# The context tile taken out of the nine-tile gather loop and run first: a hybrid mixer and expert-retrieval step on one Trainium2 core

## The reference, cut to what matters

```
m = silu(cond) @ w_mod + b_mod           # six vectors sh1, sc1, g1, sh2, sc2, g2; cond is c_ctx or c
h = rmsnorm(x, norm1) * (1 + sc1) + sh1
mix:  z = h @ w_in                       # q, f_fw, f_bw, v, g, xr, xg (512 each), ga, gb (1024 each)
      A: 4 heads, chunks of 32 tokens, forward and backward: S_t = diag(f_t) S_{t-1} + k_t v_t^T, o_t = S_t^T q_t
      B: short convolution and gated linear recurrence, forward and backward
      merged = sigmoid(ga) * (A @ w_branch_a) + sigmoid(gb) * (B @ w_branch_b);  mix = merged @ w_out
x1 = x + g1 * mix
h2 = rmsnorm(x1, norm2) * (1 + sc2) + sh2
peer: queries h2 @ w_q for 8 heads x 2 halves; scores against 128 keys each; top 16 of each half,
      top 16 of the 256 sums -> 16 experts a head, 128 rows a token, of 16384;  gate = softmax of the best sums
      act = gelu(h2 . u[e]);  out = sum_e gate_e * act_e * v[e]
y = rmsnorm(x1 + g2 * out, norm_f)
```

## Time and profile before

| | us |
|---|---|
| median of 3 runs | 4078.19 (4070.95 to 4082.48) |
| the profiled execution, its own time | 4086.17 |
| its span, first to last instruction | 4084.3 |
| end of the norm chain, start of the heads' loop on TensorE | 54.5 |
| end of the fourth head's scan, start of the merge | 735.5 |
| first gather of expert rows | 958.7 |
| last gather issued | 4057.7 |

### The profile page before, as it was taken

One profiled execution on the slowest core, in us unless ns is written; L12 is line 12 of the kernel. 1 busy time (PEld: TensorE's weight loads), 2 busy tenths in 40 slices (PEclk: granted clock), 3 DMA queues, 4 the chain that ended last, 5 costly groups with the idle time before them and its releaser, 6 DMA issues.

```text
span 4084.3 us, 44739 instructions
## 1 busy us (share of the span) xinstructions
PE 3031.6 (74%) x15406; PEld 1311.9 (32%) x15406; DVE 2613.3 (64%) x6282; ACT 1069.5 (26%) x2720; POOL 1343.0 (33%) x1174
## 2 busy tenths in 40 slices
PE   8999999798689999785666656665665665665555
PEld 3767767444344444221121111111111111111111
DVE  4545455666467667564787766776776776676555
ACT  2534435002123333111232222222222222221111
POOL 0000000002233444342444444444444444444443
PEclk9999999898899999897888877878878878787777
DMA  4010000557899999999999999999999999999998
GB/s 178 22 31 18 28 16 1 219 177 285 340 387 385 405 416 402 419 407 421 417 404 417 419 407 418 416 418 412 419 414 410 418 416 401 420 417 399 420 420 346
DMA packets 214316, 1346.40 MB, mean 330 GB/s; under 512 B 24738, under 2 KB 45730, under 8 KB 63170
## 3 DMA queue, kind: packets, MB, share of 16 engines
q0 software_dynamic: 165888, 1208.03, 71.9%
q1 hardware_dynamic: 48196, 135.41, 8.8%
HBM read 1329.69 MB, written 13.67 MB: 329 GB/s over the span
## 4 chain that ended last, share of the span: by engine, by line
PE 39%; DMA 38%; DVE 13%; issue 5%; ACT 3%; POOL 2%; POOLq 0%; SPq 0%; DVEq 0%; ACTq 0%
DMA arena<-in_uv,mask_b 13%; PE ps L760 13%; DMA arena<-in_uv,mask_f 10%; DMA arena<-in_uv,ones 10%; PE ps L1420 9%; DVE arena L1275 6%; PE ps L738 4%; PE ps L621 3%; DMA arena<-in_w_q 2%; POOL arena L599 2%; ACT arena L957 2%; PE ps L1464 2%; PE ps L1414 2%; PE ps L1481 1%; PE ps L680 1%
## 5 line engine op out<-in xcount | busy, mean ns | idle before, releaser
L760 PE MATMUL ps<-arena 64*64 64x512 f32 x9216 | 1451.7, 757 | 936.2 <-ACT arena L957 888.2
L1275 DVE CUSTOM_DVE_ANT_0 arena<-arena 128x1024 f32<-128x1024 f32 x1152 | 1412.6, 1226 | 954.5 <-DMA arena<-in_uv,mask_b 363.0
L760 PEld LDWEIGHTS ps<-arena 64*64 64x64 f32 x9216 | 350.7, 158 | 1906.2 <-ACT arena L957 1362.3
L957 ACT ACTIVATE arena<-arena 128x64 f32<-128x64 f32 x1152 | 338.2, 341 | 1411.5 <-DVE arena L1154 1411.5
L599 POOL DMA_INDIRECT arena<-in_uv,ones x384 | 449.3, 1170 | 659.7 <-PE ps L760 491.8
L599 POOL DMA_INDIRECT arena<-in_uv,mask_f x384 | 445.2, 1159 | 581.2 <-PE ps L760 493.6
L599 POOL DMA_INDIRECT arena<-in_uv,mask_b x384 | 442.3, 1152 | 584.9 <-PE ps L760 491.8
L1420 PE MATMUL ps<-arena 128*128 128x384 f32 x1152 | 387.9, 493 | 15.4 <-issue 13.5
L953 ACT ACTIVATE arena<-arena 128x2 f32<-128x2 f32 x576 | 117.5, 204 | 859.1 <-DVE arena L1275 858.4
L583 POOL IOTA arena<- 128x16 f32 x1 | 0.1, 145 | 889.5 <-PE ps L630 889.5
L738 PE MATMUL ps<-arena 128*128 128x384 f32 x768 | 270.3, 499 | 0.0
(11 more groups left out here) (205 smaller groups left out, 2836.1 us busy)
## 6 DMA issues: line engine op xcount, KB each, us to landing
arena<-in_w_mod SPq DMA_DIRECT2D x12, 2048.0 KB, 23.3
arena<-in_w_mg SPq DMA_DIRECT2D x16, 1536.0 KB, 21.8
arena<-in_w_in SPq DMA_DIRECT2D x28, 512.0 KB, 3.4
arena<-in_w_out SPq DMA_DIRECT2D x2, 4096.0 KB, 18.1
arena<-in_w_q SPq DMA_DIRECT2D x8, 1024.0 KB, 20.8
arena<-in_w_q SPq DMA_DIRECT2D x4, 2048.0 KB, 33.6
arena<-x_scratch SPq DMA_DIRECT2D x15, 512.0 KB, 11.3
arena<-in_uv,ones POOLq DMA_INDIRECT x384, 10.5
```

Source lines behind the costliest of these rows:

```text
L760: mm = nc.tensor.matmul(PS[c * HALF:(c + 1) * HALF, 2 * r + n, :], DG[rows, s, :], RG[s][rows, D + n * 512:D + (n + 1) * 512], start=(g == ...
L957: A(DG[:, s, :], halves, ACT.Copy, scale=COEF[:, s:s + 1]).then_inc(diag_r, 1)
L1275: ins = v.tensor_tensor_reduce(u, u, h2, 1.0, 0.0, ALU.mult, ALU.add, PRE[:, s % RING:s % RING + 1])
```

## The change

- The context is a group of its own (`Group(0)`), and the latent heads are groups 1 to 4 of 1024 tokens in two chunks of 512 columns. The loop over heads is written out. The latent scan has 16 steps; the context's has 8, one for each head and direction, with all four heads side by side in 512 columns. Gate products use 64x64 blocks. Parameters of all heads are loaded and worked out once.
- The context's weights come in 112 pieces of up to 512 KB through six buffers (`PIECES`, `of_piece`, `NT = 6`): w_in, w_mod, w_mg, w_out, w_q, keys. They are read a second time for the latent tokens, w_mod apart.
- Order on TensorE: context projections, three blocks of head 0, context gates and scan, two blocks of head 0, late modulation (eight blocks, now products of TensorE), context norm, merge, output product, norm, four query blocks and scores, then the scan of head 0 and heads 1 to 3, then `stage_b_pe` for eight latent tiles.
- In the scans of the heads VectorE takes items off a list (`todo`, by `between(rate)`, twice a step, a few more times in the projections; the rest at the head's end): dots of context slots (24, 32, 32, 40 in the four heads) with steps of the next context selection between them.
- GpSimd gathers u rows (512 KB each, ring of three) and, for batches whose coefficients are ready, v rows (other buffers), and scales and adds 24, 24 and 22 of them in heads 1, 2 and 3. The last 58 are added beside `merge_early`: 39 by VectorE, five before each block, 19 by GpSimd. Then `c_done` lets the loads and gathers of the latent tiles go.
- `mod_sums` and its loads leave `merge_early`. The gather loop has 8 x 64 groups. The context's end (residual, final norm) is in the loop's sixth tile.

```diff
-DVE_HEAD = 29
-GATE_STEPS = 6
-LRU_STEP = 11
+GATE_STEPS = 4
+LRU_STEP = 9
+CTX_DOTS = (24, 32, 32, 40)
+CTX_SUMS = (0, 24, 48, 70)
...
+    PIECES = [("in", b, h) for b in range(NB) for h in range(HEADS)]
+    PIECES += [("mod", c, q) for c in range(MOD1, MODC) for q in range(4)]
+    PIECES += [("mg", j, q) for j in range(KD) for q in range(3)]
+    PIECES += [("out", k, 0) for k in range(KD)]
...
+    V_BY_DVE = [s for s in V_STAGES[-1] if (s - V_STAGES[-1][0]) % 3]
+    V_BY_POOL = [s for s in range(SLOTS) if s not in V_BY_DVE]
...
-        dve.wait_ge(hg_done, HEADS)
+        dve.wait_ge(hg_done, HEADS + 1)
         for j in range(KD):
             u = j % 2
-            mod_sums(j)
+            last_batch(KD, j)
             dve.wait_ge(mg_sig, j + 1)
             merged(j, 4 * u + 2, j, slice(0, TA), TA)
...
+        last_batch(1, 0)
+        dve.wait_ge(cacc, len(V_BY_POOL))
+        v.tensor_tensor(ACC, ACC, H2C, ALU.add).then_inc(c_done, 1)
...
+        def piece(p):
+            if p >= NT:
+                sp.wait_ge(cw_used, p - NT + 1)
+            elif p < MOD1:
+                sp.wait_ge(m_ready, p + 1)
+            to, fro = of_piece(p)
+            sp.dma_start(to, fro).then_inc(l_cw[p % NT], 16)
...
+        def bias(c):
+            if c >= MOD1 + 2:
+                sp.wait_ge(md_out, 16 * (c - MOD1 - 1))
+            elif c == MOD1:
+                sp.wait_ge(t_ready, 1)
+            sp.dma_start(BR[c % 2], b_mod[:, c * 512:(c + 1) * 512]).then_inc(l_b[c % 2], 16)
+
+        def mod_out(c):
+            sp.wait_ge(m_evac, c + 1)
+            sp.dma_start(mod_d[:, c * 512:(c + 1) * 512], BR[c % 2]).then_inc(md_out, 16)
...
+        for c in range(MOD1, MODC):
+            bias(c)
+            for q in range(4):
+                piece(PIECE_AT["mod", c, q])
...
+            if c > MOD1:
+                mod_out(c - 1)
...
+        def row_load(slot, kind, s):
+            free_slot(slot)
+            slot_users[slot].append((kind, s))
+            nc.gpsimd.indirect_dma_start(
+                out=piece_(slot), out_offset=None, in_=uv_rows,
+                in_offset=bass.IndirectOffsetOnAxis(ap=EIDXC[:, s:s + 1], axis=0),
+            ).then_inc(gathered[slot], 16)
+
+        def v_add(s):
+            n, slot = V_BY_POOL.index(s), V_SLOT[s]
+            pool.wait_ge(gathered[slot], V_COUNT[s])
+            to = piece_(slot) if n else ACC
...
+            ins = nc.gpsimd.tensor_scalar(to, piece_(slot), PREC[:, s:s + 1], None, ALU.mult)
+            if n:
+                ins.then_inc(cscaled, 1)
+                pool.wait_ge(cscaled, n)
+                pool.wait_ge(cacc, n)
+                ins = nc.gpsimd.tensor_tensor(ACC, ACC, piece_(slot), ALU.add)
+            ins.then_inc(cacc, 1)
+
+        for k, vs in enumerate(V_STAGES):
+            us = CTX_BATCH[k] if k < len(CTX_BATCH) else ()
+            ahead = 3 if k < len(CTX_BATCH) else NT
+            coefs = 0
+            for n in range(max(len(us), len(vs))):
+                if n < len(us):
+                    s = us[n]
+                    if s % (2 * TOPK) == 0:
+                        pool.wait_ge(pair_done, s // (2 * TOPK) + 1)
+                    row_load(s % 3, "dot", s)
+                for x in range(ahead) if n == 0 else (n + ahead - 1,):
+                    if x < len(vs):
+                        if V_BATCH[vs[x]] != coefs:
+                            coefs = V_BATCH[vs[x]]
+                            pool.wait_ge(ccoef, coefs)
+                        row_load(V_SLOT[vs[x]], "add", vs[x])
+                if n < len(vs) and vs[n] in V_BY_POOL:
+                    v_add(vs[n])
...
+        first = G[1]
+        for bi in range(NB):
+            project_ctx(bi)
+        blocks(first, B_FF, B_Q, B_FB)
+        for gate in range(4):
+            lru_gate(C, gate, 0)
+        scan(C)
+        blocks(first, B_XR, B_V)
+        for c in range(MOD1, MODC):
+            mod_late(c)
+            if c > MOD1:
+                mod_pick(c - 1)
+        mod_pick(MODC - 1)
+        norm(C)
+        for j in range(KD):
+            merge_ctx(j)
+        out_ctx()
+        front_ctx()
+        queries_ctx(0)
...
+        def ctx_dot(s):
+            dve.wait_ge(gathered[s % 3], 16 * (s // 3 + 1))
+            u = piece_(s % 3)
+            v.tensor_tensor_reduce(u, u, H2C, 1.0, 0.0, ALU.mult, ALU.add, PREC[:, s:s + 1]).then_inc(cdots, 1)
...
+        def scan(g):
+            steps = STEPS[g.i]
+            for it, s in enumerate(steps):
+                wait_alone(dve, att_r, s.n + 1)
...
+                if it:
+                    lru(g, it - 1 - (0 if g.ctx else LRU_STEP))
+                between(rate)
+                dve.wait_ge(ds_r, s.n + 1)
...
+                if it:
+                    out_of(steps[it - 1])
+                between(rate)
+            out_of(steps[-1])
...
+        for g in LAT:
+            k = g.h
+            if g.i > 1:
+                todo.append(lambda k=k: ctx_coef(k - 1))
+            dots = [lambda s=s: ctx_dot(s) for s in CTX_BATCH[k]]
+            picks = list(Pair(-1, k + 1).steps()) if k + 1 < PAIRS else []
```

More of the change, by code:

```diff
@@ L39 @@
 CPT = P // CHUNK
-NCK = T // CHUNK
 LRU_C = 8.0
@@ new lines, in blocks, with lru_gate @@
+        def blocks(g, *bs):
+            for b in bs:
+                for n in range(NCL):
+                    project(g, b, n)
+        def lru_gate(g, gate, n):
+            if gate == 0 and n == 0:
+                pe.wait_ge(xc_r, g.i + 1)
+                if g.ctx:
+                    pe.wait_ge(l_par, 16 * 9)
+            z = free_bank(g, B_GATES + gate, n)
+            for h, sl in g.parts:
+                cols = slice(n * 512, (n + 1) * 512) if not g.ctx else sl
+                to = slice(0, 512) if not g.ctx else sl
+                for half in range(2):
+                    r = slice(half * HALF, (half + 1) * HALF)
+                    mm = nc.tensor.matmul(z[r, to], WRI[r, h, gate, :], g.XC[r, cols], start=True, stop=True)
+            mm.then_inc(z_ready, 1)
@@ L1504, in _ @@
+        queries_ctx(1)
+        turn_ctx(0)
+        score_ctx(0)
+        queries_ctx(2)
+        turn_ctx(1)
+        score_ctx(1)
+        queries_ctx(3)
+        turn_ctx(2)
+        score_ctx(2)
+        turn_ctx(3)
+        score_ctx(3)
+        pe.wait_ge(c_act, act_c("score3"))
+        for g in LAT:
+            if g is not first:
+                blocks(g, B_FF, B_Q, B_FB, B_XR, B_V)
+            scan(g)
+            norm(g)
+            pe.wait_ge(z_free, z_evacuated(g, B_SSQ))
         stage_b_pe(pe)
@@ new lines, in forgets, with values @@
+        def forgets(g):
+            forget(g, 0)
+            sums(g, 0)
+            between(rate)
+            forget(g, 1)
+            between(rate)
+            keys_(g, 0)
+            between(rate)
+            if g.i != 1:
+                sums(g, 1)
+            between(rate)
+        def values(g):
+            if g.i == 1:
+                sums(g, 1)
+            conv(g)
+            keys_(g, 1)
+            between(rate)
+        rate = 0
+        forgets(C)
+        values(C)
+        forgets(G[1])
@@ new lines, in _ @@
+        dve.wait_ge(c_act, act_c("sd"))
+        v.reciprocal(st[:, 4:5], st[:, 1:2]).then_inc(c_dve, 1)
+        dve.wait_ge(c_dve, dve_c("rstd"))
+        v.scalar_tensor_tensor(out=H2C, in0=XC1, scalar=st[:, 4:5], in1=W2C, op0=ALU.mult,
+                               op1=ALU.mult).then_inc(c_dve, 1)
+        dve.wait_ge(c_dve, dve_c("scaled"))
+        v.tensor_tensor(H2C, H2C, SH2C, ALU.add).then_inc(c_dve, 1)
+        for step in Pair(-1, 0).steps():
+            step()
+        for g in LAT:
+            k = g.h
+            if g.i > 1:
+                todo.append(lambda k=k: ctx_coef(k - 1))
+            dots = [lambda s=s: ctx_dot(s) for s in CTX_BATCH[k]]
+            picks = list(Pair(-1, k + 1).steps()) if k + 1 < PAIRS else []
+            for n, dot in enumerate(dots):
+                todo.append(dot)
+                if n % 2 and len(picks) > 1:
+                    todo.append(picks.pop(0))
+            todo += picks
+            if g.i > 1:
+                rate = 1
+                forgets(g)
+                values(g)
+            rate = 1
+            scan(g)
+            squares(g)
+            lru_end(g)
+            between(len(todo))
+            norm(g)
```

1700 lines of the change are left out of this document (1039 added, 661 removed).

## The result

The kernel after the change takes 4376.7 us (median of 4 runs, 4370.2 to 4380.5) against 4077.2 us before: the ratio is 1.073, 95% interval 1.071 to 1.075. It is 7.3% slower where 2.7% was forecast: 187 us above the forecast and 87 us above the top of the range. The profiled execution has a span of 4374.3 us at a mean clock of 0.837.

What follows compares the result with a forecast made beforehand. TensorE was taken to bound the part before the first latent gather, DMA the rest. 55 start + 346 context chain + 781 heads + 221 merge + 2793 gathers = 4196 us span, so 4190 us, 2.7% slower; range 4045 to 4290.

Steps and rivals of the forecast that it cites:

- the tile that leaves: DMA-bound gather stage: one of nine tiles leaves, worth 328 us; first gather to end becomes 2793 us.
- the context chain: Context's projections, scan, modulation, merge and output up to its first selection, run alone before the heads' scans: 346 us.
- rival 4: Gather stage: the tile that leaves isn't worth 328 us because the rest slows; 4220 us, chance 0.03.
- The late modulation: Eight context blocks on TensorE, each block's pieces waiting for the previous block's sum and store: 114 us.
- Heads 1 to 3: Latent heads paced by GpSimd's rounds beside VectorE's dots: 200, 200 and 211 us.
- the pair: GpSimd's scale and add of one value row in a round: taken at the select's rate, 1.6 us each.
- rival 1: GpSimd keeps up and selection fits VectorE's waits; heads at TensorE's pace, 160 us each; 4049 us, chance 0.17.
- 23x + 65: End of a latent head in us, with x the GpSimd round, 5.8 us taken: 198, say 200.
- The sentence on the Trainium skill, GPSIMD Engine Reference: GpSimd arithmetic: two-input operation 2.25 us for 1024 columns, one-input near line rate, 3.2 us together; streaming elementwise work advised against.
- Rival 3: Heads: VectorE and GpSimd block each other in SBUF, rounds of 7 to 8 us; 4260 to 4330 us, chance 0.12.
- The merge stage: Heads' end to first latent gather, with 58 value rows still to add: 221 us, bounds 195 and 245.
- rival 2: Heads at VectorE's pace, 170 us each, with rounds of 4.6 us or less; 4089 us, chance 0.13.

Runs made afterwards that it cites:

- e15_coef_early: Kernel after the change, with each batch's coefficients made at the end of its head instead of inside the next: 4347.6 us, ratio 1.064 to before.
- e6_sums_dve: Kernel after the change, with all 128 value rows scaled and added by VectorE, GpSimd only issuing gathers: 4123.5 us, ratio 1.011 to before.
- e1_pair_narrow: Kernel after the change, with GpSimd's scale and add on 8 of 1024 columns, so work is left out: 4042.7 us, ratio 0.989 to before.
- e12_split: Kernel after the change, every third value row on GpSimd (two-input scale), others on VectorE, two row buffers, modulation pieces requested earlier, three bias buffers: 4225.9 us.
- e9_product: Kernel after the change, with GpSimd's scale as a two-input product with the coefficient's column repeated: 4326.5 us, ratio 1.060 to before.
- e5_mod_order: Kernel after the change, with late-modulation weight pieces requested before the wait for the sum and store two blocks earlier: 4362.8 us, ratio 1.069 to before.

## Why the prediction was wrong, point by point

**The direction** was right and for the reason given: the tile that leaves is worth 328 us, the context chain that runs alone takes about as much (324), and the heads then decide.

**The tile.** First gather to end 2786.6 against 2793, last tiles 326 and 328: right, and rival 4 is out.

**The context chain** took 324 us where 346 was forecast (457.4 - 62.5, less 71 for the projections of head 0 inside it). Two terms were off, in opposite directions. The late modulation took 80 for 114. Its mechanism was right (no pieces of a block before the sum and store of the one before); two sizes were off: the store at 3.8 us, from the nearest small store, is 1.2, and a block's products, costed at 7.2 from the earlier trace rows, take 4.8 to 5.6. The context's gates and scan took 63 for 53: its steps start 5.1 us apart on TensorE, not 3.59.

```profile
185.46 0.42 PE L1673 MATMUL ps<-ident,arena 128*128 128x128 f32 x1
...
190.51 0.45 PE L1673 MATMUL ps<-ident,arena 128*128 128x128 f32 x1
```

The context's projections took 56.5 (54 forecast), normalisation and merge 53 (9 + 46), the way from the merge to the first context gather 71.4 (70). The first projection stands at 62.5 where 55 was put.

**Head 0** was to be 170 us; its projections took 71 and its scan with its end 91.4, where 93 and 6 were put: 162. That and the later start cancel.

**Heads 1 to 3.** This step failed. "Two operations at the rate of the memset ... or at that of the select" bounded the pair by 1.9 and 3.2 us; it is 5.55, and undisturbed 2.87 + 2.35 = 5.2. Both rows were of constants, of 128 columns or of a write alone: neither reads a long operand. By this alone the bounds could not hold the value, and the low forecast, the range and rival 1 all hung on them. The pair is 2.35 us above the 3.2 that was taken; 70 such pairs are 165 us, and the heads came 167 above the forecast. The round at 23x + 65 with the 8.1 to 8.4 us measured gives 251 to 258, so the formula looked right too. Both agreements are in part luck: e15_coef_early shows that the formula's start term is not how a head is built.

The sentence on the Trainium skill, GPSIMD Engine Reference, was half right. Its two-input figure, 2.25 us for 1024 columns, agrees with the 2.35 of an undisturbed add. The one-input operation near line rate (section 4.1) doesn't: 2.87 us. Where page and rows differ the rows decide. Its advice not to stream elementwise work on GpSimd agrees with e6_sums_dve.

**Rival 3** had the right side and nearly the time (4260 to 4330), but not the right cause: it had rounds of 7 to 8 us by the two engines in each other's way. They are in each other's way, but of the 88 us that a head is above VectorE's pace (259.3 - 171.4) only 14.5 go when the dots go, the dots' own length among them; most of the 88 is the arithmetic's own length, 5.2 us of the pair's 5.55. It had 0.12.

**The merge stage** was to be 221 us and was 261. By the same pair: with it narrow, 190.5. The estimate of 140 us for the value rows used 7.1 us per three rows, with the pair at 3.2.

**Rivals 1 and 2** needed rounds of 4.1 and 4.6 us. e1_pair_narrow shows what they would have brought, 4043 us; forecast for rival 1 was 4049. That nearness is luck: its heads stand at 171.4, the pace of rival 2 and not the 160 of rival 1, and the tail at 190.5 where both had 221.

## What to carry to other kernels

An operation for which the trace has no row of the same engine, the same kind of operands and a like length has no upper bound, and a range built on unlike rows has none either: such a term belongs in the range with the price of the slowest neighbour several times over, or in a small measurement first. Where two engines feed each other in program order round by round, add up one round in their order, and don't trust each one's mean load (e12_split missed by 168 us with it). And before work goes to an engine because it is idle, ask what one fused instruction on the busy one costs: here 1.28 us against 5.55.

## What the runs showed of the hardware

- GpSimd's product of one input with a factor over 1024 float columns took 2.83 to 2.99 us, the product of two inputs with a repeated column 1.94 to 1.97, and the add of two rows 2.35 when undisturbed.
- A VectorE dot beside a GpSimd add took 3.26 us, 1.23 alone (e9_product); a gather's issue that GpSimd begins while the dot runs took 1.78 us, 0.93 alone.
- A store of 4 KB was through in 1.2 us on an empty queue and in 5.2 behind 2 MB of loads of the same queue (3.4 to 7.8 in e5_mod_order).
- Where TensorE waited most, in the modulation (busy 38 of 80 us), the granted clock was 0.72. In its first block (253 to 256 us) it was 1.00, the higher of the two levels, 2.4 GHz, and an entry of a product of 512 columns (there are two a product) took 0.59 us; in its last (326.2 to 332.0 us), after a wait of 6.4 us, it was 0.50, the lower, 1.2 GHz, and an entry took 1.01 to 1.06.
